# Four expert rows of unit 14 fetched as 8 + 120 partitions and a tiny third transfer

## The reference

```python
q = (h @ w_q).reshape(B, S, PEER_HEADS, 2, PEER_HALF)
sk = jnp.einsum('bshpd,hpnd->bshpn', q, sub_keys)
top_s, top_i = lax.top_k(sk, PEER_TOPK)
...
best_s, best_pos = lax.top_k(cand_s, PEER_TOPK)
expert_idx = jnp.take_along_axis(cand_i, best_pos, axis=-1)
gates = jax.nn.softmax(best_s, axis=-1)
...
act = jax.nn.gelu(jnp.einsum('tkd,td->tk', jnp.take(u, ic, axis=0), hc))
return jnp.einsum('tk,tkd->td', gc * act, jnp.take(v, ic, axis=0))
```

## Time and profile before

| | us |
|---|---|
| median of 3 runs | 1767.48 |
| the runs | 1766.6 to 1768.01 |
| the profiled execution | 1767.52 |
| its span, first to last instruction | 1765.7 |
| PE busy | 1481.7 (84%) |
| DVE busy | 1288.1 (73%) |
| ACT busy | 545.4 (31%) |
| POOL busy | 507.1 (29%) |

### The profile page before, as it was taken

One profiled execution on the slowest core, in us unless ns is written; L12 is line 12 of the kernel. 1 busy time (PEld: TensorE's weight loads), 2 busy tenths in 40 slices (PEclk: granted clock), 3 DMA queues, 4 the chain that ended last, 5 costly groups with the idle time before them and its releaser, 6 DMA issues.

```text
span 1765.7 us, 17211 instructions
## 1 busy us (share of the span) xinstructions
PE 1481.7 (84%) x5752; PEld 879.6 (50%) x5752; DVE 1288.1 (73%) x2991; ACT 545.4 (31%) x1255; POOL 507.1 (29%) x556
## 2 busy tenths in 40 slices
PE   2999999987777878778889999999877777777787
PEld 2999976543333333233378998655333333333333
DVE  7898877667677676676579885876766766777755
ACT  3565432222222223222246663322222222222222
POOL 0000023342433334333200000343433334333330
PEclk8999999998999999998999999999999989989999
DMA  9777799999999999999957765999999999999995
GB/s 387 269 270 253 271 413 421 421 421 421 421 421 422 421 421 421 421 421 421 421 218 269 249 213 204 421 421 421 421 421 421 421 422 421 421 421 422 422 421 213
DMA packets 102616, 663.19 MB, mean 376 GB/s; under 512 B 11776, under 2 KB 11904, under 8 KB 31488
## 3 DMA queue, kind: packets, MB, share of 16 engines
q0 software_dynamic: 79488, 578.85, 79.7%
q1 hardware_dynamic: 23040, 83.26, 13.4%
HBM read 661.01 MB, written 1.05 MB: 375 GB/s over the span
## 4 chain that ended last, share of the span: by engine, by line
DMA 45%; PE 40%; DVE 11%; issue 2%; ACT 2%; SPq 1%; POOL 0%; DVEq 0%; ACTq 0%
DMA big<-pairs,big 32%; PE yac L785 16%; DMA late<-pairs,big 12%; PE acc L481 7%; PE pg L481 5%; PE acc L727 4%; DVE big L1367 2%; PE acc L651 1%; DVE big L1184 1%; DVE big L1250 1%; DVE wsp L460 1%; ACT big L998 1%; DVE big L1249 1%; DMA big<-ada 1%; PE yac L720 1%
## 5 line engine op out<-in xcount | busy, mean ns | idle before, releaser
L785 PE MATMUL yac<-big 128*128 128x512 f32 x1128 | 544.3, 631 | 100.1 <-ACT big L998 100.0
L785 PE MATMUL yac<-late,big 128*128 128x512 f32 x920 | 446.5, 632 | 123.4 <-ACT big L998 114.2
L785 PEld LDWEIGHTS yac<-big 128*128 128x128 f32 x1128 | 223.6, 202 | 402.4 <-issue 264.1
L1567 POOL DMA_INDIRECT big<-pairs,big x282 | 267.6, 949 | 405.9 <-PE yac L785 345.4
L785 PEld LDWEIGHTS yac<-late,big 128*128 128x128 f32 x920 | 178.4, 200 | 375.2 <-issue 213.0
L1567 POOL DMA_INDIRECT late<-pairs,big x230 | 217.9, 947 | 449.7 <-PE yac L785 357.4
L1367 DVE CUSTOM_DVE_ANT_0 big<-big,acc 128x1024 f32<-128x1024 f32 x148 | 179.5, 1220 | 116.0 <-DMA big<-pairs,big 115.7
L989 ACT ACTIVATE big<-big 128x4 f32<-128x4 f32 (+1 forms) x138 | 28.3, 205 | 684.1 <-DVE big L1367 684.0
L998 ACT ACTIVATE big<-con,big 128x128 f32<-128x128 f32 x512 | 164.7, 390 | 232.9 <-DVE big L1382 227.7
L1367 DVE CUSTOM_DVE_ANT_0 big<-big,pg 128x1024 f32<-128x1024 f32 x134 | 162.0, 1219 | 83.6 <-DMA big<-pairs,big 82.8
L1367 DVE CUSTOM_DVE_ANT_0 late<-late,pg 128x1024 f32<-128x1024 f32 x122 | 147.4, 1219 | 71.6 <-DMA late<-pairs,big 71.1
(11 more groups left out here) (151 smaller groups left out, 1183.9 us busy)
## 6 DMA issues: line engine op xcount, KB each, us to landing
raw<-stream SPq DMA_DIRECT2D x114, 512.0 KB
big<-ada_pairs POOLq DMA_DIRECT2D x40, 1024.0 KB, 7.7
big<-stream SPq DMA_DIRECT2D x18, 512.0 KB, 8.0
big<-ada SPq DMA_DIRECT2D x16, 512.0 KB, 13.6
big<-pairs,big POOLq DMA_INDIRECT x282, 21.8
late<-pairs,big POOLq DMA_INDIRECT x230
big<-subkeys SPq DMA_DIRECT2D x2, 1024.0 KB, 13.3
x<-xT SPq DMA_DIRECT2D x1, 1024.0 KB, 10.3
```

The costliest lines, as they stand in the source:

```text
L785: mm = pe.matmul(yac[:, 2 * t + w, :], diag(n), row(L, n)[:, D + w * 512:D + (w + 1) * 512], start=(n % (SLOTS // TT) == 0), stop=(n % (SL ...
L1567: g.indirect_dma_start(row(L, n), None, pairs, bass.IndirectOffsetOnAxis(ap=col(Q_IDX + n).bitcast(U32), axis=0)).then_inc(row_in[SLOT_OF[ ...
```

## The change

Rows 226, 230, 234 and 238 of each layer (unit 14's rows 2, 6, 10 and 14) are no longer one indirect DMA of 128 partitions but three: partitions 120 to 127 (8 rows of 8 KB), partitions 0 to 119 (120 rows of 8 KB), and a third one that fetches nine pieces of 32 bytes into a spare place in `big` that nobody reads. All three count on the row's semaphore, so that the wait for such a row is for 48 instead of 16. The index column for an indirect DMA starts at partition 0, so for the first piece the indices of partitions 120 to 127 are copied down to partitions 0 to 7, for all 16 rows of the unit at once, by a DMA of SP (8 partitions x 16 numbers) once unit 14's indices are there. POOL waits for this copy before row 226.

```diff
+APART_UNIT = 14
+APART = tuple(APART_UNIT * PICKS + n for n in (2, 6, 10, 14))
+APART_REST = 120
...
+B_ASIDE = B_SMALL + 184
...
         def rows_landed(eng, L, n):
 
             uses = USES[SLOT_OF[n]]
-            eng.wait_ge(row_in[SLOT_OF[n]], nth(L, len(uses) * 16, (uses.index(n) + 1) * 16))
+            per_layer, upto = (sum(48 if m in APART else 16 for m in part)
+                               for part in (uses, uses[:uses.index(n) + 1]))
+            eng.wait_ge(row_in[SLOT_OF[n]], L * per_layer + upto)
...
+                sp.wait_ge(index_done, L * (UNITS + 1) + APART_UNIT + 2)
+                sp.dma_start(col(B_ASIDE, PICKS)[0:P - APART_REST, :],
+                             col(Q_IDX + APART_UNIT * PICKS, PICKS)[APART_REST:P, :]).then_inc(apart_in, 16)
                 if L + 1 < depth:
                     load_next(L, CHUNKS)
                     load_next(L, CHUNKS + 1)
...
+                def fetch(out, table, index, r):
+
+                    g.indirect_dma_start(out, None, table, bass.IndirectOffsetOnAxis(ap=index, axis=0)).then_inc(
+                        row_in[r], 16)
...
-                    g.indirect_dma_start(row(L, n), None, pairs,
-                                         bass.IndirectOffsetOnAxis(ap=col(Q_IDX + n).bitcast(U32), axis=0)).then_inc(
-                        row_in[SLOT_OF[n]], 16)
+                    at = col(Q_IDX + n).bitcast(U32)
+                    if n not in APART:
+                        fetch(row(L, n), pairs, at, r)
+                        return
+                    if n == APART[0]:
+                        pool.wait_ge(apart_in, (L + 1) * 16)
+                    rest = col(B_ASIDE + n % PICKS).bitcast(U32)[0:P - APART_REST, :]
+                    fetch(row(L, n)[APART_REST:P, :], pairs, rest, r)
+                    fetch(row(L, n)[0:APART_REST, :], pairs, at[0:APART_REST, :], r)
+
+                    spare = col(B_ASIDE + PICKS + 8 * APART.index(n), 8)
+                    fetch(spare[0:9, :], pairs.rearrange("e (a b) -> (e a) b", b=8), at[0:9, :], r)
```

More of the change, by code:

```diff
@@ L176 @@
 B_SMALL = B_CACT + D
-assert B_SMALL + 184 <= B_ADA
+B_ASIDE = B_SMALL + 184
+assert B_ASIDE + PICKS + 8 * len(APART) <= B_ADA
 assert PARK_AT[3] + CH <= B_GT and PARK_AT[8] >= B_H + KD * T and 8 * ROW <= B_QP
@@ L297, in build @@
         wq_done = sem("wq_done")
+        apart_in = sem("apart_in")
         q0_done = sem("q0_done")
```

## The result

The changed kernel takes 1823.62 us, the median of four runs (1816.78 to 1824.82), against 1767.51 for the kernel before (1766.6 to 1768.01). The ratio is 1.0311, 95% interval 1.0299 to 1.0324: **slower by 56 us**. The forecast was 1756.7, with 1771 as its upper bound.

A forecast was written before the change was run, and what follows sets the result against it. The prediction took full DMA engines, with one engine about 6.7 us late ending each layer, as the bound. It summed 1767.52 - 11.4 for relief + 0.6 for small packets to 1756.7 us, range 1754 to 1771.

The forecast's parts named there:

- small packets: Split rows' extra completions and tiny packets: +0.6 us in all; pieces of partitions crossing other engines' writes: taken as nothing.
- if the relieved engine is the late one: Ends of both retrieval stages: the engine losing shares is the late one and ends 8.7 us sooner in each layer.
- the term of -11.4: Moved shares at the ends of both retrieval stages: 5.7 us gained a layer, -11.4 us over two layers.
- the third case: Rival: relieved engine is not the late one, 0 to +1.24 us a layer, 1767.5 to 1770; chance 0.15.
- The fourth case: Rival: the 8-row piece goes through one engine, adding 8.7 us a layer there, 1771.5 to 1784.9; chance 0.14.
- What bounds the kernel: Retrieval stages: DMA full at 421 GB/s sets the pace, with one engine late by about 6.7 us ending either layer.
- The worth of relieving it: Stage ends: taking shares off the late engine gains 5.7 us a layer, between 5.5 and 6.7.
- More issues: POOL: eight more DMA issues a layer, 2.5 us per split row, hidden by the engines' backlog, so cost nothing.
- tiny packets: Split rows' 32-byte pieces: 0.3 us a layer, bounded by nothing and 1.24, together +0.6 us.
- the copy and SP's queue: SP's index copy has a margin of 24 and 23 us, and loads and store behind it only move: nothing.
- Can the others follow: Last sixteen rows at 2.13 us each: DVE and PE keep up, and the tail after the last landing stays.
- the instruction fetches of the prediction's estimate: Retrieval stage: 0.29 MB of instruction fetches, if all on one engine, would make it 11 us late.

The follow-up runs named there:

- experiment 3: Changed kernel with the four rows fetched as pieces of 112 and 16 partitions, no tiny transfer, so no shares moved: 1808.09 us, ratio 1.0234.
- experiment 7: Changed kernel with only the last row of each layer (255) split, a tiny transfer of 12 ahead turning the engine placing: 1779.71 us, ratio 1.0074.
- experiment 12: Changed kernel with the four rows fetched as two transfers of all 128 partitions, 4 KB a partition each: 1768.14 us, ratio 1.0002.
- experiment 6: Changed kernel with the four rows fetched as pieces of 64 and 64 partitions, no shares moved: 1813.28 us, ratio 1.0267.
- experiment 5: Changed kernel with the engine placing turned by 12 before each of the four split rows, to relieve the late engine: 1804.64 us, ratio 1.0229.
- experiment 10: Changed kernel with four neighbouring rows (230 to 233) split instead of every fourth, placing not turned: 1803.64 us, ratio 1.0203.
- experiment 11: Changed kernel with neighbouring rows 230 to 233 split, each turned by 12 to relieve the late engine: 1779.62 us, ratio 1.0075.
- experiment 4: Changed kernel with tiny transfers ahead of split rows turning the engine placing by 9, 10, 11, 12, then 13, 14, 15, 12: 1815.3 us, one execution.
- experiment 1: Changed kernel with all rows whole again, keeping only SP's index copy and POOL's wait for it: 1766.98 us, ratio 1.0001.
- experiment 2: Changed kernel with the four rows whole, each followed by two tiny transfers (9 and 7 pieces of 32 bytes): 1767.17 us, ratio 1.0001.
- experiment 9: Changed kernel with row 226 alone split in each layer, placing not turned: 1783.14 us, ratio 1.0082.

## Why the prediction was wrong, point by point

**The step that failed first** is in *small packets*: "Since the rows carry the same bytes to the same partitions, I take nothing". Pieces of partitions cost 5.1 us a split row without any moved share (experiment 3), 41 us in all. The bound was wrong as well: "a doubled row on the loaded engines, 10 a layer", against 20 us a layer in experiment 3. It doubled the split row itself on the loaded engines, but all sixteen together fall to 213 to 231 GB/s for some 12 us a row, whole rows beside the split one included (experiment 7). Experiment 12 is what isolates it: same number of large transfers, same bytes, all partitions in both, no cost, with the two differences named there.

*Why* the packets slow down is argued, not shown. The runs that slow them differ from those that don't in which partitions a transfer covers, so in which engine writes which partitions at a time. That fits engines meeting at the same way into the on-chip memory. The Trainium skill, "SBUF — State Buffer", section "Door 1: The DMA port swizzle", says that partitions 0 to 63 reach only eight of the sixteen ports; by it a piece of 64 runs at half the rate, and experiment 6 agrees with that: 243 GB/s instead of 421 from 804 to 816. That a whole row spreads the engines evenly and a shifted piece does not would be the same mechanism for the other sizes; no record here names a port or a partition of a packet, so that stays open.

**The second step that failed** is "if the relieved engine is the late one", and with it the term of -11.4 in the sum. It is not the late one. This was the third case, given 0.15, and its price was too low as well: "0 to +1.24 a layer". It is worth 19 us between the change and experiment 5, and 24 between experiments 10 and 11. Why it is so much I only argue: the late engine, which has nine shares, does them at half the rate, and the relieved one runs 28 us ahead, so that split and whole rows overlap longer. Beside experiment 3, where nothing is moved, the change is 15 us slower and experiment 5 only 3 faster, not 11.4; in layer 1 of experiment 5 another engine became the late one.

**The fourth case** (a small piece on one engine) was slower with the wrong mechanism: by the cursor of experiment 4, 8 rows are spread over eight engines.

What held:
- *What bounds the kernel*: one late engine, the same in both layers. Experiment 4 found it by the turn at which its last completions move together.
- *The worth of relieving it*. I took 5.7 us a layer. In experiment 11 layer 0 loses 76 x (421 - 354) / 421 = 12.1 us in the window, yet its last dot stands at 896.53, only 6.7 later than before: 5.4 came back. In layer 0 of experiment 5 the same working gives 21.5 - 15.5 = 6.0. It is an estimate: in experiments 3 and 6, where nothing is relieved, the last dot is about 1 us later than the loss in the window accounts for. Where the relief worked it was sized well, and more than paid away.
- *More issues, tiny packets, the copy and SP's queue*: nothing, by experiments 1 and 2 (each within 0.1% of the kernel before). The 0.6 for the tiny packets was below what can be told.
- *Can the others follow*: nothing shows DVE or PE as the bound. PE was granted 0.50 in the stretches behind the dips, after it had waited, and the rate there was back at 387 to 414 GB/s.
- The Trainium skill, "DMA: Bandwidth & Descriptors", section "Rules for kernel authors", advises against two transfers to disjoint partition halves, and experiment 6 bears the advice out. What the prediction made of it for the time, no change, did not hold: disjoint pieces cost 5 to 8 us for each 1 MB row (experiments 3, 6 and 9).

No version here beats the kernel before. A gain would need the late engine relieved without pieces of partitions, and I tried none that does both. Why this engine is late was not tried either; the instruction fetches of the prediction's estimate remain one possibility.

## What to carry to other kernels

Cost a transfer by which partitions it covers, and not by its bytes alone: beside a full stream, pieces of consecutive partitions nearly halved the rate of everything under way, while halves by bytes over all partitions were free. Before moving work off the latest engine, find out which one it is; a row of placings that differ in one step, as in experiment 4, did it in one run. And for an access pattern that no row of the trace shows, let the upper bound count all that is in flight beside it, or measure one such transfer first: one split row would have told this change's sign.

## What the runs showed of the hardware

- The busy share of the DMA engines stayed at 1.01 to 1.03 while they moved 213 to 231 GB/s instead of 421. A full share shows occupied engines, and only the GB/s and the packets' durations (0.58 us instead of 0.313) show that they work at about half the rate.
- A split row hinders whole rows ahead of it in the queue (4.2 and 4.7 us between landings instead of 2.46, experiment 7). The engines are some 10 us, four rows, apart at that point, which fits how far ahead it reaches.
- GpSimd's indirect transfers of 8, 120 and 9 pieces each give 16 completions (48 a split row), and the completions of experiments 4 and 5 fit 8, 15 and 9 engines, which follow each other in turns.
